# A fused transformer block pair on one core: the head of the first projection reordered to go tile by tile

## What is computed

```
c_act = jax.nn.silu(c)
mod = c_act @ ada_w[l] + ada_b[l]                 # 2048 x 12288
sh_a, sc_a, g_a, sh_f, sc_f, g_f = jnp.split(mod, N_MOD, axis=-1)
h = modulate(rms_norm(x, attn_pre_norm[l]), sh_a, sc_a)   # h * (1 + scale) + shift
proj = h @ w_in
...
bias = jnp.take(bias_tab, t5_bucket(rel), axis=0)  # relative position bias, 8 heads
lam = exp(sum(lq1 * lk1)) - exp(sum(lq2 * lk2)) + lambda_init
```

## Time and profile before

| | |
|---|---|
| median of 3 runs | 1762.27 us (1761.94 to 1763.21) |
| the profiled execution | 1766.24 us |
| its span, first to last instruction | 1764.6 us |
| mean granted TensorE clock | 0.984 |
| TensorE, VectorE, ScalarE busy | 96%, 71%, 51% of the span |
| DMA | 377.11 MB, mean 214 GB/s |
| inputs of the head, KB | x 2048, c_wide 1024, positions 128 and 32, params 81.5, consts 65.5 |

### The profile page before, as it was taken

The page is one execution under the profiler, slowest core; times in us unless marked ns, Lnnn a source line. Parts: engine busy times, 40 slices in busy tenths (PEclk is TensorE's granted clock), DMA queues, the critical chain, the costliest instruction groups (busy, mean ns, idle before and its releaser), DMA issues.

```text
span 1764.6 us, 33249 instructions
## 1 busy us (share of the span) xinstructions
PE 1700.4 (96%) x13841; PEld 1657.0 (94%) x13841; DVE 1252.9 (71%) x1877; ACT 891.7 (51%) x1445; POOL 19.7 (1%) x31
## 2 busy tenths in 40 slices
PE   2899999999999999999999999999999999999997
PEld 2799999999999999999999999999899999999997
DVE  6888899898787667667667656656865676665665
ACT  8544454555565445445445435435734544446554
POOL 0000010000000000000000000000000000000000
PEclk7799999999999999999999999999999999999998
DMA  9999687788746667666666655555355444663341
GB/s 366 344 352 366 244 298 280 261 293 315 270 150 233 205 204 237 206 205 233 207 200 221 216 190 186 181 183 187 109 168 168 143 131 133 224 208 130 112 129 61
DMA packets 103109, 377.11 MB, mean 214 GB/s; under 512 B 11568, under 2 KB 11952, under 8 KB 102704
## 3 DMA queue, kind: packets, MB, share of 16 engines
q1 hardware_dynamic: 102960, 374.99, 62.3%
HBM read 372.84 MB, written 2.10 MB: 212 GB/s over the span
## 4 chain that ended last, share of the span: by engine, by line
PE 86%; DVE 7%; DMA 4%; issue 1%; ACT 1%; SPq 0%; DVEq 0%; ACTq 0%
PE ps L593 25%; PE ps L594 25%; PE ps L595 25%; DMA raw<-in_ada 3%; PE ps L714 3%; DVE raw L1562 3%; PE ps L748 1%; DVE w_lo L1552 1%; PE ps L733 1%; PE ps L756 1%; DMA raw<-in_weights 1%; PE ps L698 1%; ACT w_hi L1122 0%; PE ps L976 0%; PE ps L978 0%
## 5 line engine op out<-in xcount | busy, mean ns | idle before, releaser
L593 PE MATMUL ps<-h_hi,w_hi 128*128 128x256 f32 x3248 | 939.0, 289 | 8.8 <-DVE h_lo L1626 5.2
L594 PE MATMUL ps<-h_lo,w_hi 128*128 128x256 f32 x3248 | 921.0, 284 | 0.0
L595 PE MATMUL ps<-h_hi,w_lo 128*128 128x256 f32 x3248 | 920.8, 283 | 0.0
L1552 DVE TENSOR_TENSOR w_lo<-raw,w_hi 128x1024 fp32r<-128x1024 f32 x510 | 622.9, 1223 | 262.4 <-ACT w_hi L1122 261.2
L1122 ACT ACTIVATE w_hi<-raw 128x1024 fp32r<-128x1024 f32 x510 | 538.5, 1057 | 517.9 <-PE ps L595 474.7
L593 PEld LDWEIGHTS ps<-h_hi,w_hi 128*128 128x128 f32 x3248 | 619.9, 191 | 17.7 <-issue 11.9
L594 PEld LDWEIGHTS ps<-h_lo,w_hi 128*128 128x128 f32 x3248 | 620.4, 191 | 1.2
L595 PEld LDWEIGHTS ps<-h_hi,w_lo 128*128 128x128 f32 x3248 | 620.1, 191 | 0.0
L1562 DVE SCALAR_TENSOR_TENSOR raw<-raw,c_wide 128x2048 f32<-128x2048 f32 x96 | 219.5, 2288 | 21.3 <-DMA raw<-in_ada 21.2
L593 PE MATMUL ps<-g_hi,w_hi 128*128 128x256 f32 x704 | 199.5, 283 | 0.6 <-DVE conv L1960 0.6
L594 PE MATMUL ps<-g_lo,w_hi 128*128 128x256 f32 x704 | 199.4, 283 | 0.0
(11 more groups left out here) (237 smaller groups left out, 1213.2 us busy)
## 6 DMA issues: line engine op xcount, KB each, us to landing
raw<-in_weights SPq DMA_DIRECT2D x510, 512.0 KB, 3.7
raw<-in_ada SPq DMA_DIRECT2D x192, 512.0 KB, 5.6
x<-in_x SPq DMA_DIRECT2D x1, 2048.0 KB, 12.9
out_y<-x SPq DMA_DIRECT2D x3, 512.0 KB, 2.9
c_wide<-in_c_wide SPq DMA_DIRECT2D x1, 1024.0 KB, 5.1
consts<-in_consts SPq DMA_DIRECT2D x1, 798.0 KB, 10.1
out_y<-x SPq DMA_DIRECT2D x2, 256.0 KB, 2.6
params<-in_params SPq DMA_DIRECT2D x1, 504.0 KB, 8.6
```

The lines of the kernel that those rows point to most:

```text
L593: nc.tensor.matmul(out, wh, hi[:, k, :], start=start, stop=False)
L594: nc.tensor.matmul(out, wh, lo[:, k, :], start=False, stop=False)
L595: last = nc.tensor.matmul(out, wl, hi[:, k, :], start=False, stop=stop)
L1552: V.tensor_tensor(w_lo[:, h % W_SLOTS, :], raw[:, raw_slot("w", h), :], w_hi[:, h % W_SLOTS, :].bitcast(F32), ALU.subtract).then_inc(lo_dv ...
```

## The change

The first 8 units of the first pass are no longer made one by one but together, tile by tile: for each of feature tiles 0 to 7, all eight units' products of that tile are made (24 matmuls), with one half of weights that now holds tile k of eight units. They lie two to a bank in banks 0, 1, 4 and 5. The stream alternates: one half of weights, then the scale's and the shift's item of the same tile. The shift's items of tiles 1, 3, 5 and 7 are laid out with inputs on the partitions and summed by TensorE (16 matmuls of one column each, `shift_product`) with `c_act`, a Silu of c by columns. VectorE's loop takes, for each tile: lo, one or two sums, the scale's column, the scaled tile, the shift's column, h_lo. ScalarE's loop takes, for each tile: hi, h_high, eight masks (tiles 0 to 3), and copies of the position bias. The position bias is summed in banks 2 and 3 alone, in four turns, the second and third inside the loop, the fourth behind unit 11. `x` and `c_wide` are issued behind params and consts and ahead of the whole stream. The exponential for lambda goes behind the early units. The idle matmuls go.

```diff
 # order of the modulation's items and of the loads
-ADA = ([(v, t) for b in range(2) for v in (SC_A, SH_A) for t in range(SLAB * b, SLAB * b + SLAB)]
+ADA = ([(v, t) for t in range(SLAB) for v in (SC_A, SH_A)]
+       + [(v, t) for v in (SC_A, SH_A) for t in range(SLAB, KT)]
...
-    out = a(0, 8) + w(0, 2) + a(8, 16) + w(2, 4)
-    out += spread(w(4, 31), a(16, 32)) + w(31, 35)
+    out = []
+    for t in range(SLAB - 1):
+        out += w(t, t + 1) + a(2 * t, 2 * t + 2)
+    out += w(SLAB - 1, SLAB + 1) + a(2 * SLAB - 2, 2 * SLAB)
+    out += spread(w(SLAB + 1, 31), a(16, 32)) + w(31, 35)
...
 # SyncE
-                        sp.wait_ge(ada_used, i + 1)
+                        if i // 2 in PE_RANK:
+                            sp.wait_ge(shift_summed, PE_RANK[i // 2] + 1)
+                        else:
+                            sp.wait_ge(ada_used, 2 * DVE_RANK[i // 2] + 2)
...
-            for n in range(2 * RAW_SLOTS + 2):
-                load(n)
+            sp.dma_start(c_wide[:, :, :].rearrange("p a b -> p (a b)"), A["c_wide"]).then_inc(inputs_loaded[7], 16)
             sp.dma_start(x[:, :, :], A["x"]).then_inc(inputs_loaded[4], 16)
...
 # TensorE
+            def shift_product(t):
+                i = ADA_AT[SH_A, t]
+                pe.wait_ge(silu_col, 1)
+                pe.wait_ge(*loaded("a", 2 * i))
+                pe.wait_ge(*loaded("a", 2 * i + 1))
...
+                for k in range(KT):
+                    last = nc.tensor.matmul(out, raw[:, at + k // TILES, P * (k % TILES):P * (k % TILES) + P],
+                                            c_act[:, k:k + 1], start=k == 0, stop=k == KT - 1)
+                last.then_inc(shift_summed, 1)
+
+            def early_products(k):
+                pe.wait_ge(*lo_done(k))
+                pe.wait_ge(h_ready, HN["x0"] + k + 1)
+                for u in range(EARLY):
...
+                    nc.tensor.matmul(out, wh, h_hi[:, k, :], start=k == 0 and u % 2 == 0, stop=False,
+                                     skip_group_check=True)
+                    nc.tensor.matmul(out, wh, h_lo[:, k, :], start=False, stop=False, skip_group_check=True)
+                    last = nc.tensor.matmul(out, wl, h_hi[:, k, :], start=False, stop=k == SLAB - 1,
+                                            skip_group_check=True)
...
-            for i in range(3):
-                bias_sums(i)
-            pe.wait_ge(lam_exp, 1)
-            bias_sums(3)
-            pe.wait_ge(bias_ready, 6)
+            bias_sums(0)
             mean_square("x0", KT)
...
+            widen("x0")
+            for k in range(SLAB):
+                if k in (2, 5):
+                    bias_sums(1 + k // 5)
+                if k % 2:
+                    shift_product(k)
+                early_products(k)
+            for j in range(EARLY, N_IN):
+                unit(U_IN + j, range(SLAB), h_hi, h_lo)
+                if j == 11:
+                    bias_sums(3)
             pe.wait_ge(bias_ready, 8)
-            widen("x0")
-            keep_going(H_IN, 6)
...
 # ScalarE
+            for part in range(2):
+                signs(part)
             act.wait_ge(inputs_loaded[4], 16)
             squares("x0", KT, lambda k: x[:, k, :])
             root("x0")
...
+            for k in range(SLAB):
+                hi(H_IN + k)
+                act.wait_ge(shift_made, k + 1)
+                h_high("x0", SH_A, [k])
+                if k < 4:
+                    signs(k + 2)
+                if k in (0, 1, 3, 4, 6):
+                    for n in {0: [0], 1: [1], 3: [2], 4: [3], 6: [4, 5]}[k]:
+                        bias_out(n)
+            for k in range(SLAB, SLAB + 3):
+                hi(H_IN + k)
+            for u in range(0, EARLY, 2):
+                early_evac(u)
+            hi(H_IN + SLAB + 3)
...
 # VectorE
+            for k in range(SLAB):
+                scale, shift = ADA_AT[SC_A, k], ADA_AT[SH_A, k]
+                lo(H_IN + k)
+                ada(scale)
+                if not on_pe(shift):
+                    ada(shift)
...
+                chain.link(V.scalar_tensor_tensor(out=col, in0=mod_raw[:, SC_A, k:k + 1], scalar=col,
+                                                  in1=par("attn_pre", k, 1), op0=ALU.add, op1=ALU.mult))
+                dve.wait_ge(wide_ready, WIDE_AT["x0"])
...
+                V.scalar_tensor_tensor(out=normal_in(k), in0=x[:, k, :], scalar=col, in1=wide("x0"), op0=ALU.mult,
+                                       op1=ALU.mult).then_inc(modulated, 1)
...
+                V.tensor_tensor(mod[:, SH_A, k:k + 1], raw_shift, par("ada_b", SH_A * KT + k, 1), ALU.add
+                                ).then_inc(shift_made, 1)
...
+                dve.wait_ge(h_hi_ready, k + 1)
+                V.scalar_tensor_tensor(out=h_lo[:, k, :], in0=normal_in(k), scalar=mod[:, SH_A, k:k + 1],
+                                       in1=h_hi[:, k, :].bitcast(F32), op0=ALU.add, op1=ALU.subtract
+                                       ).then_inc(h_ready, 1)
             item = 16
-            for j in range(4, N_IN):
+            for j in range(EARLY, N_IN):
                 lo(H_IN + j)
```

More of the change, by code:

```diff
@@ L128, in make_banks @@
         else:
-            b = (0, 1, 4, 5)[u % 4]
+            b = (0, 1, 4, 5)[u // 2 if u < EARLY else u % 4]
         bank.append(b)
@@ L801, in _ @@
             pe.wait_ge(lam_prod, 1)
-            nc.tensor.matmul(ps[:, OUT + 1, 0:2], mean_mat[0:64, :], lam[0:64, 0:2], start=True,
-                             stop=True).then_inc(lam_sum, 1)
+            nc.tensor.matmul(ps[:, NORM_BANK["x0"], LAM_COLUMN:LAM_COLUMN + 2], mean_mat[0:64, :], lam[0:64, 0:2],
+                             start=True, stop=True).then_inc(lam_sum, 1)
             def bias_sums(i):
                 pe.wait_ge(bias_mask, i + 1)
+                if i:
+                    pe.wait_ge(bias_ready, 2 * i)
                 for qt in range(2):
@@ L827, in _ @@
             last.then_inc(row_turned, 1)
+            widen("x0")
[9 more added lines that the diff above has]
+                    bias_sums(3)
             pe.wait_ge(bias_ready, 8)
-            widen("x0")
-            keep_going(H_IN, 6)
-            for j in range(N_IN):
-                unit(U_IN + j, range(SLAB), h_hi, h_lo, (h_ready, HN["x0"], SLAB) if j == 0 else None)
             def diff(a):
@@ L1255, in _ @@
             act.wait_ge(start_ready, 1)
-            for i in range(3):
-                signs(i)
-            for h in range(2):
-                hi(H_IN + h)
-            signs(3)
-            act.wait_ge(lam_sum, 1)
-            nc.scalar.activation(lam[:, 2:4], ps[:, OUT + 1, 0:2], ACT.Exp).then_inc(lam_exp, 1)
-            for n in range(6):
-                bias_out(n)
+            for part in range(2):
+                signs(part)
             act.wait_ge(inputs_loaded[4], 16)
@@ new lines, in _ @@
+                if on_pe(shift):
+                    dve.wait_ge(shift_summed, PE_RANK[shift] + 1)
+                    raw_shift = ps[:, NORM_BANK["x0"], SHIFT_COLUMN + k:SHIFT_COLUMN + k + 1]
+                else:
+                    ada_made(shift)
+                    raw_shift = mod_raw[:, SH_A, k:k + 1]
+                V.tensor_tensor(mod[:, SH_A, k:k + 1], raw_shift, par("ada_b", SH_A * KT + k, 1), ALU.add
+                                ).then_inc(shift_made, 1)
+                dve.wait_ge(shift_made, k + 1)
@@ L1841, in _ @@
                     ada(item)
                     item += 1
-                if j == 8:
+                if j == 12:
                     angles()
+                    dve.wait_ge(lam_exp, 1)
+                    chain.link(V.tensor_tensor(lam[:, 4:5], lam[:, 3:4], lam[:, 2:3], ALU.subtract))
+                    chain.link(V.tensor_scalar(lam[:, 4:5], lam[:, 4:5], -LAMBDA_INIT, None, ALU.add))
                 elif j == 25:
-                    mod_out(2)
+                    mod_out(0)
                     for k in range(SLAB, SLAB + 4):
@@ L2322, in _arrays @@
     ada = i["ada_w"][0].reshape(2, HALF, 6, KT, P)[:, :, ADA_ORDER]
-    ada = np.stack([ada[b, :, v, t].T for v, t in ADA for b in range(2)])
+    ada = np.stack([ada[b, :, v, t].reshape(TILES, P, P).transpose(1, 0, 2).reshape(P, HALF) if on_pe(n)
+                    else ada[b, :, v, t].T for n, (v, t) in enumerate(ADA) for b in range(2)])
     return {
```

118 lines of the change are left out of this document (70 added, 48 removed).

## The result

The changed kernel is slower: 1809.37 us (median of 4 runs, 1808.23 to 1814.07) against 1762.11 for the kernel before on the same chip, a ratio of 1.0274 with a 95% interval of 1.0261 to 1.0287. That is +47.3 us where +36.5 were forecast; 1809 lies in the range of 1783 to 1814. A second job with the same kernel gave 1806.46 against 1761.51, 1.0258 (1.0244 to 1.0272).

The account below looks back on a forecast made before the run. TensorE, 96% busy, was taken as the bound, so only its idle time could be won. Steps and later units put the first pass's end at 194.8 against 158.3: +36.5 us on 1762.3, so 1799, range 1783 to 1814.

Parts of the forecast that it names:

- Until the first step: Start of the kernel through masks, squares, root and first sums to the end of tile 0's h_hi, at 37.0 us.
- One step: Loop from h_hi(k) to h_hi(k+1): ScalarE and VectorE alternate, 5.2 us (4.3 without bias copies) plus 4.9 or 7.2.
- T5: End of tile 5's h_hi, 94.2 us; TensorE last: products 4.8, bias sums 2.75, shift sums 3.7.
- The last step: Tile 7: load 40 waits on SP's queue behind load 39 for lo(7), lands at 112.6; shift sums take 5 us.
- T7: End of tile 7's h_hi, the last of the loop, at 118.4 us.
- Unit 8: Behind the loop: waits for bank 0, emptied only behind hi(10), which needs w10's landing; ready at 125.8 us.
- The stretch of the units 8 to 30: After the loop, at TensorE's pace: 23 units x 2.88 = 66.2 us, plus fourth bias sums 2.75, ending at 194.8.
- The clock: TensorE's bursts in the loop mostly start at half clock; by the skill each costs 5.1 us instead of 2.9.
- The stream sets the pace: Rival for the head: only bytes count, steps under 6.4 us; 15.5 us less than before, 1747; chance 0.05.
- Waits less than added: Rival: TensorE and transfers never last, +24; with ScalarE pieces hidden +8 to +18, 1770 to 1781; chance 0.08.
- more than added: Rival: half-clock squares +3.2, table load +1.3, shift sums +6, ring stalls +5; +52, 1814; chance beyond that 0.05.
- The products do not overlap at all: Rival: bank or weight slots hold the loop's products, each step 3 to 5 us more, 1825; chance 0.01.

Follow-up runs that it names:

- e1: Changed kernel with ScalarE making hi(k+1) right behind h_hi(k), ahead of masks and bias copies; 1795.31 us, 1.0192 of the kernel before.
- e11: The changed kernel repeated unaltered in another job; 1806.46 us, 1.0258 of the kernel before.
- e10: Changed kernel with the copy of bank 0 (units 0 and 1) ahead of hi(10); 1807.64 us, 1.0266 of the kernel before.
- e5: Changed kernel with the load of w8 moved behind item 15 of the modulation; 1798.99 us, 1.0205 of the kernel before.
- e6: Changed kernel with eight modulation items of units 8 to 30 neither loaded nor summed, but copied from neighbours; 1801.25 us, 1.0217 of the kernel before.
- e4: Changed kernel with idle matmuls on TensorE ahead of tiles 2, 4 and 7; 1802.10 us, 1.0232 of the kernel before.
- e7: Changed kernel with early hi, all sums on VectorE and run ahead, loads reordered to match, bank 0 copied earlier; 1759.79 us, 0.9981 of the kernel before.
- e9: e7 with the loads of units 8 to 30 issued in VectorE's order of use; 1757.82 us, 0.9978 of the kernel before.

## Why the prediction was right

The mechanism and the sign stood: between ends of h_hi, forecast and measured (start in the timeline and 0.4 to 0.5):

| tile | 0 | 1 | 2 | 3 | 4 | 5 | 6 | 7 |
|---|---|---|---|---|---|---|---|---|
| forecast | 37.0 | 47.1 | 59.5 | 69.3 | 81.7 | 94.2 | 102.5 | 118.4 |
| measured | 37.1 | 47.6 | 59.6 | 70.1 | 82.0 | 96.7 | 104.6 | 122.5 |

- *Until the first step:* 37.0 and 37.1, in part by luck, since two misses cancelled. c_wide was the fifth issue and not the fourth, so its Silu started at 8.73 where I had 7.7, and the masks and TensorE's bias sums ended some 0.9 later; but four squares went ahead of the wait for those sums (17.03 to 18.35), where I had all sixteen behind them. The squares went in 0.43 each, and the Sign after the root needed no table load: 0 of the two ends was right.
- *One step:* right to 0.8 us up to tile 4. The alternation was the cause, as e1 shows by undoing it (VectorE's wait 20.7 to 2.8, 13.1 us at the second pass).
- *Tile 1 was TensorE's too.* I priced step 1 by the other two engines; its shift sums took 4.75 (42.25 to 47.0) and ended last. It cost 0.5. "Behind products I take 3.7" was too low in every odd step (4.75, 4.06, 5.43), since the clock fell within the sums each time. The windows of the first of them:

```profile
42.20:44.50 2.30, 2.30 (x23) 2.30 (x23) 2.30 (x2) 0.00 (x0) 0.00 (x0) 1.00 0.14 14
44.50:47.00 2.50, 2.50 (x13) 2.42 (x12) 1.81 (x4) 0.00 (x0) 0.00 (x0) 0.51 0.60 202
```

- *T5, the first term whose miss was large:* "shift sums 3.7" behind the bias sums. They took 5.43 here, 5.36 in e11 and 5.32 in e10, and 3.77 and 3.76 in e5 and e6: the clock fell early in them here and only near their end there. Two windows of the changed kernel, then one of e5 in the same sums:

```profile
90.60:93.00 2.40, 2.40 (x26) 2.40 (x22) 0.00 (x0) 0.00 (x0) 0.00 (x0) 0.86 1.04 418
93.00:96.00 3.00, 3.00 (x15) 2.97 (x14) 0.00 (x0) 0.00 (x0) 0.00 (x0) 0.50 0.08 29
```

```profile
90.20:92.00 1.80, 1.80 (x23) 1.80 (x19) 0.00 (x0) 0.00 (x0) 0.00 (x0) 1.00 1.02 419
```

  With all 24 products ahead of them at the half clock as well, T5 came 14.7 behind T4 where I had 12.5.
- *The last step:* "shift sums after a rest, between 3.7 and 7.4, I take 5". They took 6.96, near the doubled price, since the half clock held for the whole of it: +2.0. The item landed at 114.8 (109.51 and 5.27) where I had 112.6: of those 2.2, lo(7) ended 1.9 later, by what T5 had added, and the ring's rule (load 40 waits behind load 39 for lo(7)) was right, which e5 shows by moving w8 (3.1 us from tile 5 to tile 7). Together T7 is 4.1 later than forecast.
- *Unit 8:* 7.4 us behind T7 forecast, 7.6 measured; the cause was the one given, the copy of bank 0 behind hi(10) behind w10, but e10 shows that it hid a wait of 2.8 for the masks that the prediction had costed at nothing.
- *The stretch of the units 8 to 30, the term that failed most:* 23 units x 2.88 + 2.75 = 69 forecast, 77.4 measured. I took TensorE's own pace and named the two others as near (186 to 196); they were not near but last in places. Of the 8.4 us, 2.2 are waits for w_lo, 2.3 the wait for h_lo at the second pass (0.9 of which I had beside the sum), 0.4 the masks, and what stood behind two of the waits: TensorE went on for some 3.5 us at half clock. The windows of the changed kernel behind its waits at 130 and 177.5:

```profile
177.50:181.60 4.10, 4.06 (x21) 4.09 (x22) 4.10 (x4) 2.30 (x3) 0.00 (x0) 0.58 0.99 353
130.00:134.00 4.00, 3.93 (x21) 3.94 (x22) 2.37 (x2) 3.88 (x7) 0.00 (x0) 0.59 1.04 416
```

21 matmuls in 4 us where the full clock gives 33 or 34 (4.0 and 4.1 over 0.12): 1.5 to 1.7 us lost each time, 3.2 together. With the waits that makes 8.1 of the 8.4. e6 confirms the stretch by halving its items (77.4 to 71.3).

The sum of the misses: 4.1 + 0.2 + 8.4 = 12.7, and 194.8 + 12.7 = 207.5. Of it the kernel before has 0.9 ahead of its own second pass, which leaves 11.8 (48.3 - 36.5); in the medians it is 47.3 - 36.5 = 10.8.

- *The clock.* Seven of the eight bursts started at half clock, as the one burst of before did after its rest at 65.0: products 0.21 us apart for 3 to 5 us, then 0.12 for what was left, if any. That of tile 6 started at 0.12 and fell to 0.21 after four matmuls. In the prediction it was worth 0.9 us since only products were counted; e4 puts the clock at 5 to 7 us, with up to 1.7 and 1.2 of them in the shift sums of steps 5 and 7. By the rule of the Trainium skill ("TensorE: Matmul & The Clock Gate", section "HAM oscillation — how this bites in real kernels"), a tile starts cold where the work of the one before is shorter than the wait. The trace agrees in steps 4 and 7, where the rest (6.92 and 4.89) was longer than the products before it. Ahead of the products of tiles 1, 3 and 5 the rest was only 1.47, and the clock had already fallen within the one-column sums, with TensorE busy; that is outside the rule.
- *The rivals.* "The stream sets the pace" fell for this kernel (DMA share 0.57), but e7 shows it as what would have been with the queues in another order: steps of 6.7 us against my 6.4. Only its end was wrong: it gave 15.5 us less than before, while e7 has 2.7. I had left out that the units behind the head need the same stream. "Waits less than added" fell. Of "more than added" the last step's sums at 7 and the ring's stalls came true, the squares and the table load did not. "The products do not overlap at all" fell.

What stays open: why e7 and e9 are 2.7 and 3.7 us faster than before by their medians, while their second pass starts 0.1 later and 3.3 earlier than in the profile of before. That profile is from an execution with TensorE's pace 0.4% lower, and there is no other of before, so I can't say where before's head ends in the executions that it is compared with. What makes the clock fall early in step 5's sums in three executions and late in two is open as well. A deeper ring of slots, or the masks on another engine, were not tried.

## What to carry to other kernels

Where work is made finer so that it overlaps a transfer, write out one step for every queue, with what stands between two dependent operations on each: here a 1.1 us operation stood behind 4.1 us of filler that nothing needed yet, and moving it ahead (no work less) was worth 13 us. Then ask what the stretch behind has to carry: e7 has its first tile 32 us before the kernel before and wins 3, with a DMA share of 0.95 from 2 to 155 us in both. Price sums of one column on TensorE at both clocks, and at the slower one if what precedes them is a wait for a load; here even the lower price, 3.6 us, was above VectorE's 2.29.
